# One core of Trainium2, a two-layer encoder trunk: the S5 output in three parts, the S5 input in one batch, the first gate-matrix block by itself, and a matrix preparation in four pieces

## The reference, cut to what matters

```python
def _s5_mixer(u, a_re, a_im, b_re, b_im, c_re, c_im, d_skip, log_dt, w_glu):
    ...
    bu_re = jnp.einsum('blgi,gni->blgn', ug, bb_re)
    bu_im = jnp.einsum('blgi,gni->blgn', ug, bb_im)
    ... # a complex diagonal recurrence over the L positions, by an associative scan
    y = jnp.einsum('blgn,gin->blgi', x_re, c_re) - jnp.einsum('blgn,gin->blgi', x_im, c_im)
    y = y.reshape(B, L, S5_WIDTH) + d_skip * u
    y = jax.nn.gelu(y)
    return y * jax.nn.sigmoid(y @ w_glu)

y_s5 = (_s5_mixer(s_in, ...) * jax.nn.silu(s_gate)) @ w_s5_out[layer]
```

## Time and profile before

| | |
|---|---|
| three runs | 1935.65, 1940.91, 1940.92 us (median 1940.91) |
| profiled execution | 1936.7 us, of which the profiled span is 1934.8 us |
| mean granted TensorE clock | 0.961 of full speed |
| busy share of the span | TensorE 92%, its weight loads 82%, VectorE 50%, GpSimd 40%, ScalarE 36% |
| chain that ended last, by engine | TensorE 63%, VectorE 10%, DMA 8%, GpSimd 6%, SP's queue 6%, ScalarE 4% |

### The profile page before, as it was taken

One profiled execution on the slowest core, in us unless ns is written; L12 is line 12 of the kernel. 1 busy time (PEld: TensorE's weight loads), 2 busy tenths in 40 slices (PEclk: granted clock), 3 DMA queues, 4 the chain that ended last, 5 costly groups with the idle time before them and its releaser, 6 DMA issues.

```text
span 1934.8 us, 29460 instructions
## 1 busy us (share of the span) xinstructions
PE 1774.6 (92%) x12239; PEld 1588.4 (82%) x12239; DVE 969.9 (50%) x1527; ACT 694.5 (36%) x1236; POOL 782.0 (40%) x478
## 2 busy tenths in 40 slices
PE   6976898999998997989998999989999899799997
PEld 5876798999988996988997977777788687678886
DVE  8996134333429882467653203533333698635223
ACT  3453432444533221332324543344455221223322
POOL 2644665333323322533331786544332322334442
PEclk8898999999999998999998999999999999999999
DMA  9455244222254544535552333532223655523432
GB/s 146 142 164 152 79 104 117 81 68 66 65 146 142 181 138 100 104 82 177 157 163 85 99 87 88 132 93 77 76 61 72 176 172 179 110 77 98 140 101 87
DMA packets 356043, 221.77 MB, mean 115 GB/s; under 512 B 49604, under 2 KB 346744, under 8 KB 353352
## 3 DMA queue, kind: packets, MB, share of 16 engines
q1 hardware_dynamic: 345384, 189.75, 37.5%
q10 hardware_dynamic: 10528, 30.15, 4.6%
HBM read 172.17 MB, written 38.50 MB: 109 GB/s over the span
## 4 chain that ended last, share of the span: by engine, by line
PE 63%; DVE 10%; DMA 8%; POOL 6%; SPq 6%; ACT 4%; issue 3%; ACTq 0%; DVEq 0%; POOLq 0%
PE ring L794 45%; DMA sb_w_raw<-in_w_in 4%; POOL sb_w_lo L650 3%; PE ring L775 3%; PE ring L753 2%; PE aux L1037 2%; PE aux L1129 2%; DVE sb_s_prod L1515 1%; DVE sb_s_mat_prod L1515 1%; SPq L559 1%; DMA sb_w_raw<-in_w_s_out 1%; PE aux L1116 1%; SPq L525 1%; SPq L606 1%; DVE sb_s_gelu_lo L1515 1%
## 5 line engine op out<-in xcount | busy, mean ns | idle before, releaser
L650 POOL TENSOR_TENSOR sb_w_lo<-sb_w_raw,sb_w_hi 128x1024 fp32r<-128x1024 f32 x246 | 607.0, 2470 | 1067.3 <-ACT sb_w_hi L1181 1065.1
L1181 ACT ACTIVATE sb_w_hi<-sb_w_raw 128x1024 fp32r<-128x1024 f32 x246 | 259.9, 1057 | 654.5 <-DMA sb_w_raw<-in_w_in 409.6
L794 PE MATMUL ring<-sb_u_hi,sb_w_hi 128*128 128x264 f32 (+1 forms) x2112 | 358.7, 322 | 21.3 <-ACT sb_att_q L1223 11.0
L794 PEld LDWEIGHTS ring<-sb_u_hi,sb_w_hi 128*128 128x128 f32 x2112 | 304.8, 196 | 52.6 <-ACT sb_att_q L1223 12.6
L794 PE MATMUL ring<-sb_u_lo,sb_w_hi 128*128 128x264 f32 (+1 forms) x2112 | 338.4, 311 | 0.0
L794 PE MATMUL ring<-sb_u_hi,sb_w_lo 128*128 128x264 f32 (+1 forms) x2112 | 334.5, 309 | 0.0
L794 PEld LDWEIGHTS ring<-sb_u_lo,sb_w_hi 128*128 128x128 f32 x2112 | 298.5, 191 | 21.7
L794 PEld LDWEIGHTS ring<-sb_u_hi,sb_w_lo 128*128 128x128 f32 x2112 | 294.0, 188 | 21.1
L1213 ACT ACTIVATE sb_tmp_act<-ring 128x528 f32<-128x528 f32 (+1 forms) x112 | 67.5, 602 | 143.8 <-PE ring L794 103.3
L1437 ACT ACTIVATE sb_att_scores<-sb_att_scores,sb_att_neg_max 128x208 f32<-128x208 f32 x128 | 58.5, 458 | 90.8 <-DVE sb_att_neg_max L1800 90.8
L794 PE MATMUL ring<-sb_y_hi,sb_w_hi 128*128 128x264 f32 (+1 forms) x504 | 88.1, 325 | 3.2 <-ACT sb_w_hi L1181 3.1
(11 more groups left out here) (320 smaller groups left out, 2591.6 us busy)
## 6 DMA issues: line engine op xcount, KB each, us to landing
sb_w_raw<-in_w_in SPq DMA_DIRECT2D x166, 512.0 KB, 4.1
sb_s_loaded<-s_matrices ACTq DMA_DIRECT2D x16, 1808.0 KB, 7.5
s_matrices<-sb_s_phase SPq DMA_DIRECT2D x16, 528.0 KB, 3.2
s_matrices<-sb_s_mbt SPq DMA_DIRECT2D x16, 512.0 KB
s_matrices<-sb_s_ca SPq DMA_DIRECT2D x16, 512.0 KB
sb_w_raw<-in_w_gla_out SPq DMA_DIRECT2D x16, 512.0 KB, 4.1
sb_w_raw<-in_w_attn_out SPq DMA_DIRECT2D x16, 512.0 KB, 4.0
sb_w_raw<-in_s_w_glu SPq DMA_DIRECT2D x16, 512.0 KB, 4.2
```

Source lines behind the costliest of these rows:

```text
L650: pool.tensor_tensor(WL[:, w], WR[:, w], WH[:, w].bitcast(F32), ALU.subtract).then_inc(lo_ready, 1)
L794: last = pe.matmul(RING[:, 2 * r + hf, 0:c1 - c0], w[:, n % SLOTS, kt, :], moving(b[0], xx[:, kt], c0, c1), start=(term == 0 and kt == 0), ...
L1181: act.activation(WH[:, w], WR[:, w], ACT.Copy).then_inc(hi_ready, 1)
```

## The change

S5_IN goes from 3 to 2, and all 16 input DMAs are issued at block 0. The S5 output no longer goes back to Z: it has a buffer of its own, YZ, in the memory of the attention queries (AQ, free once the ag blocks are read), and goes there in three parts of 16 DMAs each, for channel groups 0 to 3 at block 14, 4 and 5 at block 18, 6 and 7 at block 21, with a semaphore for each part. GH moves to the place of Z. ScalarE makes GH for the first two parts after block 20 and for the third after block 21; VectorE makes GL at blocks 21 and 22. glu 0 runs alone, following GL; glu 1 to 7 are plain blocks. The second layer's first matrix set is one generator of four pieces, taken after sg 2, 3, 4 and 5; its C transposes go from sg 5 to sg 2. Buffers of the second matrix set and of the merged output's high part change places.

```diff
-S5_IN = 3
-S5_OUT = {S5_IN + 3 + 2 * j: j for j in range(KT)}
-S5_YT, S5_SPLIT = 21, 22
+S5_IN = 2
+S5_OUT = {6 + 2 * j: j for j in range(KT)}
+S5_YT = {14: (0, 4), 18: (4, 6), 21: (6, 8)}
+S5_SPLIT = {21: ((0, 4), (4, 6)), 22: ((6, 8),)}
+YT_PARTS = list(S5_YT.values())
...
-MATS_1 = [("sg", 5)] + [("ws5", j) for j in (0, 1, 2, 3, 5)] + [("wout", j) for j in (0, 2, 4)]
+MATS_1 = [("sg", 2)] + [("ws5", j) for j in (0, 1, 2, 3, 5)] + [("wout", j) for j in (0, 2, 4)]
...
-        GH = sb("s5_gelu_hi", [P, KT, L], F32R, at=[o_aq, o_aq + WIDE])
+        GH = sb("s5_gelu_hi", [P, KT, L], F32R, at=[base, base + WIDE])
+        YZ = sb("s5_out", [P, KT, STRIDE, STEPS], at=[o_aq, o_aq + WIDE])
...
-              mat_buffers(1, [o_aq, o_aq + WIDE], [o_att, end])]
+              mat_buffers(1, [base, base + WIDE], [o_att, end])]
...
-        MXH = sb("mix_hi", [P, KT, L], F32R, at=[base, end])
+        MXH = sb("mix_hi", [P, KT, L], F32R, at=[o_aq, o_aq + WIDE])
...
-                    if name in (("ag", 0), ("ag", 1)):
-                        for q in (2 * name[1], 2 * name[1] + 1):
+                    if name == ("ag", 0):
+                        for q in range(QUADS):
                             for p in range(STRIDE):
                                 sp.dma_start(Z4[32 * p:32 * p + 32, :, q, :],
                                              Z[32 * q:32 * q + 32, :, STRIDE - 1 - p, :]).then_inc(
                                                  steps_loaded, 16)
-                    if name == S5F[S5_YT]:
-                        aux_read(sp, ly, ("y", 6))
-                        aux_read(sp, ly, ("y", 7))
+                    if name in S5F and S5F.index(name) in S5_YT:
+                        j0, j1 = S5_YT[S5F.index(name)]
+                        aux_read(sp, ly, ("y", j1 - 2))
+                        aux_read(sp, ly, ("y", j1 - 1))
                         for q in range(QUADS):
                             for t in range(STRIDE):
-                                sp.dma_start(Z[32 * q:32 * q + 32, :, t, :],
-                                             Z4[32 * t:32 * t + 32, :, q, :]).then_inc(yt_loaded, 16)
+                                sp.dma_start(YZ[32 * q:32 * q + 32, j0:j1, t, :],
+                                             Z4[32 * t:32 * t + 32, j0:j1, q, :]
+                                             ).then_inc(yt_loaded[YT_PARTS.index((j0, j1))], 16)
...
-                project_two_as_made(ly, (("glu", 0), ("glu", 1)), GH, GL, ylo_ready, 32 * ly + 16)
-                for j in range(2, KT):
+                project_as_made(ly, ("glu", 0), GH, GL, ylo_ready, 32 * ly + 16)
+                for j in range(1, KT):
                     project(ly, ("glu", j), GH, GL)
...
-                            if i == S5_SPLIT:
-                                act.wait_ge(yt_loaded, 256 * ly + 256)
-                                for j in range(KT):
-                                    act.activation(GH[:, j], zs[j], ACT.Copy).then_inc(yhi_ready, 1)
+                            if i + 1 in S5_SPLIT:
+                                act.wait_ge(x_state, 8 * ly + 8)
+                                for part in S5_SPLIT[i + 1]:
+                                    act.wait_ge(yt_loaded[YT_PARTS.index(part)], 256 * ly + 256)
+                                    for j in range(*part):
+                                        act.activation(GH[:, j], YZ[:, j].rearrange("p s c -> p (s c)"), ACT.Copy
+                                                       ).then_inc(yhi_ready, 1)
...
-                            if i == S5_SPLIT:
-                                for t in range(KT):
+                            for part in S5_SPLIT.get(i, ()):
+                                for t in range(*part):
                                     dve.wait_ge(yhi_ready, 32 * ly + 16 + t + 1)
-                                    tt(GL[:, t], Z[:, t].rearrange("p s c -> p (s c)"), GH[:, t].bitcast(F32),
+                                    tt(GL[:, t], YZ[:, t].rearrange("p s c -> p (s c)"), GH[:, t].bitcast(F32),
                                        ALU.subtract).then_inc(ylo_ready, 1)
...
-                    if ly == 0 and b == ("sg", 3):
-                        input_matrix(1)
+                    if ly == 0 and b == ("sg", 2):
+                        first_set = itertools.chain(input_matrix(1), s5_matrices(1, 0))
+                    if ly == 0 and kind == "sg" and 2 <= j <= 5:
+                        next(first_set)
                     if ly == 0 and b in MATS_AFTER and MATS_AFTER[b][0] == 1:
                         k = MATS_AFTER[b][1]
-                        if k < KT:
-                            s5_matrices(1, k)
-
+                        if 0 < k < KT:
+                            for _ in s5_matrices(1, k):
+                                pass
```

More of the change, by code:

```diff
@@ L7 @@
+import itertools
 import math
@@ L361, in trunk @@
         phase_spilled, zeroed = sem("phase_spilled"), sem("zeroed")
-        yt_loaded = sem("yt_loaded")
+        yt_loaded = [sem(f"yt_loaded{i}") for i in range(3)]
         out_ready, out_stored = [sem(f"out_ready{i}") for i in range(2)], sem("out_stored")
@@ L600, in _ @@
                                                  steps_loaded, 16)
[L601 to L603 removed]
+                    if name in S5F and S5F.index(name) in S5_YT:
+                        j0, j1 = S5_YT[S5F.index(name)]
+                        aux_read(sp, ly, ("y", j1 - 2))
+                        aux_read(sp, ly, ("y", j1 - 1))
                         for q in range(QUADS):
                             for t in range(STRIDE):
[L606 to L607 removed]
+                                sp.dma_start(YZ[32 * q:32 * q + 32, j0:j1, t, :],
+                                             Z4[32 * t:32 * t + 32, j0:j1, q, :]
+                                             ).then_inc(yt_loaded[YT_PARTS.index((j0, j1))], 16)
                     if name == ("mg1", 3):
[L609 removed]
+                        for part in yt_loaded:
+                            sp.wait_ge(part, 256 * ly + 256)
                         produced(sp, ly, ("glu", KT - 1))
@@ L1488, in _ @@
                                 load_mats(ly, i // 2)
-                            zs = [Z[:, j].rearrange("p s c -> p (s c)") for j in range(KT)]
-                            if i == S5_SPLIT:
-                                act.wait_ge(yt_loaded, 256 * ly + 256)
-                                for j in range(KT):
-                                    act.activation(GH[:, j], zs[j], ACT.Copy).then_inc(yhi_ready, 1)
+                            if i + 1 in S5_SPLIT:
[5 more added lines that the diff above has]
+                                                       ).then_inc(yhi_ready, 1)
             link(act.activation(WARM[:, 0:1], ONES[:, 0:1], ACT.Sqrt))
@@ L1638, in gla_gates @@
                         pass
-                    input_matrix(0)
-                    s5_matrices(0, 0)
+                    for _ in input_matrix(0):
+                        pass
+                    for _ in s5_matrices(0, 0):
+                        pass
                 def decay(hd):
@@ L1664, in matrices @@
                         for j in js:
-                            s5_matrices(0, j)
+                            for _ in s5_matrices(0, j):
+                                pass
                 decay(0)
@@ L1928, in input_matrix @@
                 t = [BT[:, i].rearrange("p (q i) -> p q i", i=S5_GROUP) for i in range(2)]
-                complex_mult(BB[:, 0], BB[:, 1], bc[0], bc[1], SB_[:, 0], SB_[:, 1], t[0], t[1])
+                tt(t[0], bc[0], SB_[:, 0], ALU.mult)
+                link(tt(t[1], bc[1], SB_[:, 1], ALU.mult))
+                link(tt(BB[:, 0], t[0], t[1], ALU.subtract))
+                yield
+                tt(t[0], bc[0], SB_[:, 1], ALU.mult)
+                link(tt(t[1], bc[1], SB_[:, 0], ALU.mult))
+                link(tt(BB[:, 1], t[0], t[1], ALU.add))
                 if m == 0:
```

7 lines of the change are left out of this document (4 added, 3 removed).

## The result

| | |
|---|---|
| changed kernel, 18 runs | median 1917.71 us (1908.37 to 1934.28) |
| kernel before, 18 runs | median 1937.65 us (1932.56 to 1944.40) |
| ratio | 0.9903, 95% interval 0.9882 to 0.9924 |

The change saves about 20 us where 43 were forecast; 1917.7 lies above the range. In the changed kernel L1585, L1620, L1129 and L775 of before are L1594, L1629, L1136 and L760; step_inputs is L1123, the low part L657, and L1524 is VectorE's helper for tensor_tensor (L1515 before).

The account below looks back on a forecast made before the run. TensorE, 92% busy, was taken as the bound, with gains only where it waits or runs at its lower clock. 15.4 + 14.0 + 12.5 + 1 = 42.9 off 1936.7 gave 1893.8 us, predicted as 1894, range 1880 to 1912.

Parts of the forecast that it names:

- The start of S5: All input DMAs at block 0 start the scan earlier; TensorE's stall moves to ag 4's slot; 12.5 us gained, bounds 5 and 22.4.
- delayed the load of ag 4 and slowed that of ag 3: At the S5 start: what eight input DMAs at block 1 on SP's queue did to weight loads; no separate size given.
- weights no longer late: At the S5 start: argument that the change ends late weights, set against a rival with a gain of 5 instead of 12.5.
- rival B: S5 start gains little, 5 instead of 12.5 us, as VectorE's list is the bound; nothing from pieces; 1902.3 us; chance 0.14.
- The bound without idle: Upper bound at the S5 start without any idle at ag 6: gains of 9.5 and 12.9, given as 22.4 us.
- So nothing is lost: At blocks 14 and 18: output DMAs delay the next weight load, 4.4 us at block 14, but TensorE needs it later; cost none.
- Rival E: No change that can be told: output parts one and two make step_inputs wait, 42 us go again; 1935 us; chance 0.03.
- The handover: Before glu: output in three parts and glu 0 alone shorten TensorE's wait; gains 15.4 and 14.0 us in the two layers.
- both are short enough for the full clock: Before glu 0: remaining waits of 1.3 and 2.1 us in the two layers leave TensorE's clock at its full rate.
- Rival D: Slower: each output DMA holds its queue until landed, glu 0 some 40 us later in each layer; 2003 us; chance 0.03.
- The pieces: Second layer's first matrix set in four pieces: one 5.3 us stall becomes several shorter ones; 1 us gained, bounds 0 and 8.
- The memory moves: Moved buffers, with the shorter list in glu 0, cost nothing: same sizes, and what they replace was read earlier.

Follow-up runs that it names:

- only_start: Kernel before with only the S5 start changed (S5_IN = 2, all sixteen input DMAs at block 0): ratio 0.9996 to the kernel before.
- mats_later: load_split with ag 0 to 4's low parts at block 5, tanh before high part for ag 1 and 2, second matrix load after block 4, not 2: 0.9819.
- load_tanh_defer: Changed kernel, weight loads before output DMAs at blocks 14 and 18, ag 0 to 4's low parts at block 5, tanh before high part for ag 1, 2: 0.9840.
- start_order: only_start with the low parts of ag 0 to 4 at block 5 and tanh before the high part for ag 1 to 5: 0.9924, 1922.6 us.
- order_only: Kernel before with only low parts of ag 0 to 4 at block 5 and tanh before the high part for ag 1 to 5: 0.9969, 1930.1 us.
- load_split: Changed kernel, weight loads before output DMAs at blocks 14 and 18, half of the third part's DMAs on ScalarE's queue: 0.9808, in a later batch 0.9839.
- load_defer: Changed kernel with weight loads before output DMAs at blocks 14 and 18, and the low parts of ag 0 to 4 at block 5: 0.9842.

## Why the prediction was wrong

**The start of S5 is the step that failed**: 12.5 us forecast, 1.4 in the trace, nothing in the ratio of only_start. The sentence that failed is that the eight input DMAs at block 1 "delayed the load of ag 4 and slowed that of ag 3", and with it "weights no longer late", my argument against rival B. Its first half held: the wait of 4.50 us for ag 4's weights went. Its second half is wrong: the 9.59 us of the earlier trace rows go with the 1.8 MB matrix load, issued within 0.1 us of ag 3's weights, and they stayed 9.55 when the input DMAs no longer followed them. No run moves this first matrix load; that it is the cause is taken from mats_later, which moves the second, and from the landing times of all traces. I had the wait in a row, and named the wrong neighbour for it.

From the first product to the freed slot of ag 4 I gave 18.4 us; it was 17.1. The place of the new stall, the slot of ag 4 before ag 6, was right; its size, 3.1 us, came out as 5.8 in the change, where the scan began 5 us late; the three VectorE operations beside GpSimd's low parts took 4.5 us more than 0.71 each.

An early beginning alone doesn't cure it: in load_tanh_defer the scan began at 20.2 us, and the list behind it took 22.2 us with the wait for the tanh of ag 3 in its middle. start_order, in which the tanh passes these waits, gained 14.7 us; order_only gained 6.0 of that without the earlier start. So the time was there, but not by the change's edits. Rival B came true in its result, but not by its cause alone: VectorE's list was the bound as long as ScalarE's waits for weights stood in front of it or in its middle. (The bound without idle sums to 22.1 us and not 22.4; nothing hangs on that.)

**"So nothing is lost" for blocks 14 and 18 failed too**, by 2.9 + 3.3 us. The late weights of block 21 did not hold TensorE, as I worked out; I asked only whether they come in time, not what their low part runs beside. In the first layer before, the state was ready 0.46 us before step_outputs(7). In the change two groups of products that meet a low part take 4.3 us more, and the two rotations, which met one before, take 1.33 us in place of 2.29; what is left, 2.9 us, is about the wait of 2.81. Rival E named the place (DMAs make the S5 steps late) but not this path.

**The handover was right in its mechanism and too large in its size**: 23.7 us in place of 29.4. Issue 10.84 us (10.2 assumed), landing 4.0 (4.2), the waits 2.0 and 2.3 (1.3 and 2.1). What is missing besides lies in the clock: "both are short enough for the full clock" held in the first layer (1.00) and not in the second (0.66, glu 0 to sg 0 45.9 us against 44.3 in load_split), and after the new wait on the state step_outputs(7) itself ran slowly (its first group 1.25 us against 0.61, at a granted clock of 0.68 from 720 to 725). Doing glu 0 alone was worth some 7 to 11 us; I had not separated it from the parts. Rival D stayed far off: the third part's sixteen DMAs each landed 1.9 us (median) after their issue while the next went out 0.68 us later.

**The pieces** gained 2.4 us (1 assumed, bounds 0 and 8), with waits of 2.91 and 1.22 us in place of 0.4 and 5.3. **The memory moves** cost nothing that shows.

In sum: 42.9 - 5.7 (handover) - 11.1 (start) - 6.2 (waits on the state) + 1.4 (pieces) = 21.3 us.

Left open: why executions of one kernel differ by up to 26 us, and by up to 10 in stages that no edit touches, and why load_defer's shorter stage does not show in its ratio. Part of the spread can be placed: between the changed kernel's execution of 1934.28 us and that of 1913.39, 9.4 us lie between step_outputs(1) and (6) of the first layer, with two more waits of 2.8 us on the state, and 3.9 in that layer's handover, where a wait of 3.09 us was followed by a granted clock of 0.50 over 5 us; 6.7 lie ahead of the first ag 0.

## What to carry to other kernels

When a wait ends on a late transfer, look for every transfer issued within the same microsecond, largest first, before the wait is put down to one of them; moving another changes nothing. When a load may come later because it is needed late, ask also which engine converts it, and beside which instructions of the other engine that shares its port. An earlier start pays only if everything that stands in front of the chain and between its steps, in each engine's queue, comes earlier with it.
